# Router logits of a hybrid block: token activations as the stationary operand, 36 router columns moving

## The chip, the core and the metric

The kernel runs on one core of one Trainium2 chip. The metric is the device time of one execution in microseconds (us), as the median of several runs. The profile is one execution, recorded by the hardware profiler.

## What is computed

One decoder block on 256 tokens of width 1024, in float32. A gated short convolution and an attention run on the same input, are merged and projected (`mix`); then a layer norm, a hierarchical mixture of experts and a second layer norm follow. Cut to what matters here:

```python
x = layer_norm(alpha * x + mix, ln1_g, ln1_b)
g_prob = softmax(xt @ w_router_group)                 # (256, 4)
g_top_p, g_top = top_k(g_prob, 1)
e_logits = (xt @ w_router_expert).reshape(-1, 4, 8)   # (256, 32)
e_top_logit, e_top = top_k(e_logits[g_top], 2)        # two experts inside the group
...
h = silu(xt @ w_gate[e]) * (xt @ w_up[e]) * combine   # 32 experts, width 256
ffn = h @ w_down[e]
x = layer_norm(alpha * x + ffn, ln2_g, ln2_b)
```

The router is a product of the (256, 1024) activations with 4 + 32 = 36 columns.

## The kernel before

The 256 tokens are two tiles (`TT = 2`) of 128, and the width 1024 is eight chunks (`KC = 8`) of 128. Everything is written out by hand for each engine, and the engines meet at semaphores; an engine takes its instructions in the order of the program.

**Up to the router.** TensorE (PE) computes the projections; the mix is added up in banks 0 to 3 of PSUM (`merge`, L1366), and ScalarE (ACT) copies it out as `zx` (L760), tokens on partitions. VectorE (DVE) takes mean and variance, GpSimd (POOL) the reciprocal root `rstd`. The first layer norm is not applied before the router: its gain and bias are folded into the router's weights `wr` (36 columns with the gain, then 36 with the bias), and the mean is brought in by `offs`, so that a logit is `rstd * (zx @ wr) + offs`.

**The router.** `transpose_tile` (L1398) turns `zx` into chunks with channels on partitions, in banks 4 and 5 for tile 0 and 6 and 7 for tile 1; four copies on ACT (L765) make `x1T` of them and count `bank_free[4]` to `bank_free[7]`. `logit_parts(t)` (L1409) then loads 36 columns of `wr` for each chunk as the stationary operand and moves 128 tokens of `x1T` past them. Even chunks are summed in partitions 0 to 35 of bank `4 + t`, odd ones in partitions 64 to 99 (`APART_AT`), so the result lies with logits on partitions and in two parts. `take_parts` (L1003, DVE) copies it to `lT`, and `logits` (L1416, PE) multiplies `lT` as the stationary operand by `both`, two shifted pieces of the identity added together, which turns the result back to tokens on partitions and adds the two parts. L1037 (DVE) reads that and adds `offs`.

**Behind the router.** DVE finds the best group and two experts in a chain of short instructions (L1021 to L1052), PE counts ranks (L1435), DVE makes one-hot selections `pick` (L1070), and PE starts the experts: gather with `pick` (L1450), gate and up products (L1501), down product (L1537), scatter (L1549), in quads of four experts, eight quads. Between L1416 and L1435 PE also zeroes the four sums (`zero_sums`, L1242) and runs nine products for warmth (L1303).

**Loads.** All large loads go through one queue in SyncE's (SP) order. At the router this is, from the code:

```python
sp.wait_ge(acc_done, 2 * TT)
load_gu(1, 1, [3], parts=[1])
sp.wait_ge(parts_ps, TT)
load_gu(1, 1, [2], parts=[1])
sp.wait_ge(offs_read, TT)
load_dn_early(3, slice(0, 1))
sp.wait_ge(x1p_done, TT)
load_gu(1, 1, [0], parts=[0])
```

The tile `gu` for the next quad and `dn_r` overlay tiles that the router still uses (`x1T`, `wr`, `offs`), which is why these loads wait. `x1p` (L771, ACT) is the normalized activation, for the gather. After that SP waits for `rounds_done` and for `gate_ps`, counted by the first gate products, to refill the buffer of quad 0 with quad 2's weights in three pieces (L533), then for `gu_ps` and `y_ps` of each quad.

Of the kernel before, what the change touches and what calls it, by code (L numbers as in the profile page):

```python
# [27 lines left out]
ALU = mybir.AluOpType  # L28
# [3 lines left out]
P = 128  # L32
SEQ, DM = 256, 1024
TT = SEQ // P
# [41 lines left out]
def hybrid_block(nc, x, w_in, conv_w, w_out_conv, w_out_attn, w_o, ln1_g, ln1_b,  # L76
# [18 lines left out]
    with ctx:  # L95
        def sb(name, shape, dt=F32, where=ctx):
            return where.enter_context(nc.sbuf_tensor(name, shape, dt))

        def sem(name):
            return ctx.enter_context(nc.semaphore(name))  # L100
# [92 lines left out]
        y_scope.close()  # L193
        lT_scope = ExitStack()
        lT = sb("lT", [P, TT, P], where=lT_scope)
        lT_scope.close()
        xg_scope = ExitStack()
# [55 lines left out]
        rounds_f = sb("rounds_f", [P, 4, 16], where=route_scope)  # L253
        both = sb("both", [P, NL], where=route_scope)
        route_scope.close()
# [81 lines left out]
        x1T_ps = sem("x1T_ps")  # L337
        parts_ps = sem("parts_ps")
        lT_done = sem("lT_done")
        logit_ps = sem("logit_ps")  # L340
# [50 lines left out]
        UPJ = 8  # L391
        APART_AT = P // 2
        AHEAD = NSPL - 2
# [18 lines left out]
        def _(sp):  # L412
# [103 lines left out]
            load_gu(1, 1, [3], parts=[1])  # L516
            sp.wait_ge(parts_ps, TT)
            load_gu(1, 1, [2], parts=[1])
# [305 lines left out]
        def _(dve):  # L824
# [70 lines left out]
            def scale_router():  # L895

                dve.wait_ge(consts, N_CONSTS)
                dve.wait_ge(small_in, N_SMALL)
                dve.tensor_tensor(both[:, :], ident[:, 0:NL], ident[:, APART_AT:APART_AT + NL], ALU.add)
                for v, cols in ((wrg, slice(0, NG)), (wre, slice(NG, NL))):  # L900
# [98 lines left out]

            def take_parts(t):  # L1000

                dve.wait_ge(parts_ps, t + 1)
                dve.tensor_copy(lT[:, t, :], bank[4 + t][:, 0:P]).then_inc(lT_done, 1)  # L1003

            take_parts(0)
            dve.wait_ge(neg_mean_done, 1)
            dve.wait_ge(bias_read, 1)
            for t in range(TT):
                ins = dve.scalar_tensor_tensor(offs[:, t, :], rsum_b[:, 0:NL], neg_mean[:, t:t + 1],
                                               rsum_b[:, NL:2 * NL], ALU.mult, ALU.add)  # L1010
            take_parts(1)
            link(ins)
# [21 lines left out]
            gtop, tmp, gsum, w1, w2 = (rs[:, i, :] for i in range(5))  # L1034
            dve.wait_ge(logit_ps, 1)
            for t in range(TT):
                ins = dve.scalar_tensor_tensor(logit[:, t, :], bank[4][:, t * NL:(t + 1) * NL],  # L1037
                                               rstd[:, t:t + 1], offs[:, t, :], ALU.mult, ALU.add
                                               ).then_inc(offs_read, 1)
# [153 lines left out]
        def _(pe):  # L1193
# [208 lines left out]

            def logit_parts(t):

                for k in range(KC):
                    if t and k % KHALF == 0:
                        pe.wait_ge(bank_free[6 + k // KHALF], 1)
                    at = APART_AT * (k % 2)
                    mm = pe.matmul(bank[4 + t][at:at + NL, 0:P], wr[:, k, 0:NL], x1T[:, k, t * P:(t + 1) * P],  # L1409
                                   start=(k < 2), stop=(k >= KC - 2), skip_group_check=True)  # L1410
                mm.then_inc(parts_ps, 1)

            def logits(t):

                pe.wait_ge(lT_done, t + 1)
                return pe.matmul(bank[4][:, t * NL:(t + 1) * NL], lT[:, t, :], both[:, :],  # L1416
                                 start=True, stop=True, skip_group_check=True)

# [3 lines left out]
            for b in (4, 5):  # L1422
                pe.wait_ge(bank_free[b], 1)
            logit_parts(0)
            logit_parts(1)
            logits(0)
            logits(1).then_inc(logit_ps, 1)
            pe.wait_ge(moment_done, TT)
# [186 lines left out]
```

## Time and profile before

| | |
|---|---|
| median of 3 runs | 391.53 us (391.07 to 392.49) |
| profiled execution | 391.15 us |
| its span, first to last instruction | 388.7 us |
| outside the span | 2.45 us |
| PE busy | 359.8 us (93%) |
| DVE busy | 161.4 us (42%) |
| ACT busy | 138.6 us (36%) |
| HBM read | 131.25 MB, 340 GB/s over the span |

The busy share of PE is an average over stages with different limits, and it includes products that only keep the engine warm. An engine name "PEld" is the load of the stationary operand, which the profile lists apart from the product. One float32 product is two records on PE and two on PEld where it is a true product, so `x32` at L1409 is 16 products; a transpose is one record.

### The profile page before, as it was taken

How to read it: one execution, taken by the hardware profiler on the slowest of the kernel's cores; microseconds unless marked ns; L12 is line 12 of the kernel's file. 1: busy time of each engine (PE TensorE's matmuls, PEld its weight loads, DVE VectorE, ACT ScalarE, POOL GpSimd, SP SyncE). 2: the span in 40 equal slices, each digit the busy share in tenths (PEclk: the TensorE clock that was granted, in tenths of full speed). 3: DMA queues.
4: the chain of work that ended last, by engine and by line, in shares of the span. 5: the costliest groups of instructions: out<-in, count | busy, mean ns of one | idle time of the engine just before them, and what ended most of it. 6: DMA issues, size and time to landing. Idle time of an engine off the chain costs nothing.

```text
span 388.7 us, 8033 instructions
## 1 busy us (share of the span) xinstructions
PE 359.8 (93%) x3336; PEld 285.8 (74%) x3336; DVE 161.4 (42%) x336; ACT 138.6 (36%) x240; POOL 35.2 (9%) x42
## 2 busy tenths in 40 slices
PE   7999999999999999999999999999599598299995
PEld 6999988999999999998657575656256356157642
DVE  3546579787365666464731202030510112011135
ACT  4643565655535453435723131322111213012012
POOL 3310000000000000001000005208720000000001
PEclk9999999999999999999999999999799899599999
DMA  8699884966859879799899999999999999999962
GB/s 284 211 329 375 292 303 156 337 221 218 275 177 316 274 265 376 239 389 368 311 385 429 424 427 425 417 420 427 427 420 414 427 426 426 427 424 429 411 256 110
DMA packets 52053, 132.79 MB, mean 342 GB/s; under 512 B 2818, under 2 KB 36626, under 8 KB 41012
## 3 DMA queue, kind: packets, MB, share of 16 engines
q1 hardware_dynamic: 51572, 131.88, 87.9%
q8 instruction: 26, 0.43, 0.4%
q0 software_dynamic: 304, 0.17, 0.4%
q10 hardware_dynamic: 144, 0.26, 0.2%
q14 instruction: 7, 0.06, 0.0%
HBM read 131.25 MB, written 1.05 MB: 340 GB/s over the span
## 4 chain that ended last, share of the span: by engine, by line
PE 70%; DMA 13%; DVE 6%; SPq 4%; issue 3%; ACT 3%; DVEq 0%
PE bank L1204 15%; PE bank L1501 13%; PE bank L1233 7%; DMA gu<-in_w_up 7%; PE bank L1537 7%; PE bank L1366 6%; PE bank L1450 6%; PE bank L1549 6%; DMA raw<-in_w_in 5%; SPq L470 4%; PE bank L1236 3%; DVE wl L837 3%; PE bank L1303 2%; ACT wh L655 1%; PE bank L1520 1%
## 5 line engine op out<-in xcount | busy, mean ns | idle before, releaser
L837 DVE TENSOR_TENSOR wl<-raw,wh 128x1024 fp32r<-128x1024 f32 x54 | 65.8, 1223 | 54.6 <-ACT wh L655 54.5
L1501 PE MATMUL bank<-gu,xg 128*32 128x256 f32 x1024 | 63.4, 407 | 17.8 <-issue 17.7
L655 ACT ACTIVATE wh<-raw 128x1024 fp32r<-128x1024 f32 x54 | 56.5, 1056 | 61.2 <-DMA raw<-in_w_in 23.4
L1501 PEld LDWEIGHTS bank<-gu,xg 128*32 128x32 f32 x1024 | 35.0, 117 | 42.5 <-issue 23.8
L1233 PE MATMUL bank<-xh,wh 128*128 128x256 f32 x176 | 44.1, 288 | 0.1
L1233 PE MATMUL bank<-xl,wh 128*128 128x256 f32 x176 | 43.1, 283 | 0.0
L1233 PEld LDWEIGHTS bank<-xh,wh 128*128 128x128 f32 x176 | 33.6, 191 | 2.3 <-issue 2.0
L1101 DVE TENSOR_SCALAR xg<-bank,gcol,bcol 128x128 f32<-128x128 f32 x32 | 11.7, 406 | 53.6 <-PE bank L1450 53.6
L1233 PEld LDWEIGHTS bank<-xl,wh 128*128 128x128 f32 x176 | 33.7, 191 | 0.0
L1450 PEld LDWEIGHTS bank<-pick,x1p 128*128 128x128 f32 x256 | 29.9, 192 | 2.4 <-issue 1.3
L1450 PE MATMUL bank<-pick,x1p 128*128 128x128 f32 x256 | 30.5, 276 | 0.7 <-DVE pick L1070 0.7
L1549 PE MATMUL bank<-ys,put 128*128 128x256 f32 (+1 forms) x96 | 30.0, 461 | 0.7 <-ACT ys L796 0.7
L1549 PEld LDWEIGHTS bank<-ys,put 128*128 128x128 f32 x96 | 17.4, 189 | 13.6 <-issue 10.1
L1204 PE MATMUL bank<-xh,wl 128*128 128x256 f32 x96 | 27.2, 283 | 0.0
L1204 PE MATMUL bank<-xl,wh 128*128 128x256 f32 x96 | 27.2, 283 | 0.0
L1204 PE MATMUL bank<-xh,wh 128*128 128x256 f32 x96 | 27.2, 283 | 0.0
L780 ACT ACTIVATE xg<-bank,bcol,gcol 128x128 f32<-128x128 f32 x32 | 13.7, 456 | 34.5 <-PE bank L1450 34.5
L1537 PE MATMUL bank<-dn,hT 128*32 128x256 f32 (+1 forms) x324 | 25.9, 453 | 0.0
L1236 PE MATMUL bank<-xh,wl 128*128 128x256 f32 x176 | 24.7, 283 | 0.0
L1236 PEld LDWEIGHTS bank<-xh,wl 128*128 128x128 f32 x176 | 22.7, 192 | 0.0
L1127 DVE TENSOR_TENSOR sg<-sg,bank 128x256 f32<-128x256 f32 x8 | 3.4, 421 | 41.7 <-ACT sg L786 41.7
L786 ACT ACTIVATE sg<-bank 128x256 f32<-128x256 f32 x8 | 3.1, 384 | 48.1 <-PE bank L1501 48.1
(228 smaller groups left out, 586.6 us busy)
## 6 DMA issues: line engine op xcount, KB each, us to landing
gu<-in_w_up SPq DMA_DIRECT2D x31, 1024.0 KB, 19.0
gu<-in_w_gate SPq DMA_DIRECT2D x30, 1024.0 KB, 14.5
dn<-in_w_down SPq DMA_DIRECT2D x26, 1024.0 KB, 17.7
raw<-in_w_in SPq DMA_DIRECT2D x40, 512.0 KB, 5.2
raw<-in_w_o SPq DMA_DIRECT2D x8, 512.0 KB, 4.4
raw<-in_w_out_conv SPq DMA_DIRECT2D x4, 512.0 KB, 4.2
raw<-in_w_out_attn SPq DMA_DIRECT2D x4, 512.0 KB, 5.5
gu<-in_w_gate SPq DMA_DIRECT2D x1, 2048.0 KB, 9.9
```

The costliest lines, as they stand in the source:

```text
L470: sp.dma_start(gu[(NQ - 1) % 2][:, e, c, ks, :], (wg_v, wu_v)[c][:, (NQ - 1) * QE + e, ks, :]).then_inc(last_up_end if i else last_gu_in[c ...
L655: act.activation(wh[:, s, :].rearrange("p (k c) -> p k c", k=KC), raw[pair % NRAW][:, :].rearrange("p (k c) -> p k c", k=KC) [:, :, n % 2 ...
L780: act.activation(xg[:, k, :], bank[XG_BANK[i]][:, (k - lo) * P:(k - lo + 1) * P], ACT.Identity, scale=gcol[:, k:k + 1], bias=bcol[:, k:k + ...
L837: dve.tensor_tensor(wl[:, s, :].rearrange("p (k c) -> p k c", k=KC), raw[pair % NRAW][:, :].rearrange("p (k c) -> p k c", k=KC) [:, :, n % ...
L1204: mm = pe.matmul(dst, w[:, k, :], v[:, i, :], start=(i == 0 and w is h and v is high_in), stop=(i == len(ks) - 1 and w is l))
L1233: pe.matmul(dst, h[:, k, :], v[:, k, :], start=(k == 0 and v is xh), stop=False)
L1236: mm = pe.matmul(dst, l[:, k, :], xh[:, k, :], start=False, stop=(k == KC - 1))
L1366: mm = pe.matmul(bank[2 * t + h][:, :], v[:, m, t * P:(t + 1) * P], w[:, s, h * HALF:(h + 1) * HALF], start=(j == 0 and m == 0 and i == 0) ...
L1450: mm = pe.matmul(bank[XG_BANK[i]][:, (k - lo) * P:(k - lo + 1) * P], x1p[:, t, k, :], pick[:, t, :, :].rearrange("p e s -> p (e s)"), star ...
L1501: mm = pe.matmul(bank[6 - part][g, 0:DE], xg[:, k, g], w[:, e, part, k, :], start=(k == 0), stop=(k == KC - 1), skip_group_check=True)
L1537: mm = pe.matmul(bank[b][g, 0:hi - lo], hT[:, j, g], dn_of(q, e)[:, j, lo:hi], start=(j == 0), stop=(j == FC - 1), skip_group_check=True)
L1549: pe.matmul(bank[2 * t + lo // HALF][:, lo % HALF:lo % HALF + hi - lo], put[:, t * P:(t + 1) * P], ys[:, lo:hi], start=False, stop=True, s ...
```

## The change

`logit_parts`, `take_parts`, `lT` and `both` are gone. `logits(t)` now takes a chunk of `x1T` (128 channels, 128 tokens) as the stationary operand and moves the 36 columns of `wr` past it. The eight products of a tile add up in one place, the first 36 columns of bank `4 + t`, with tokens on partitions already. `logit_ps` is counted once per tile, and both SP's load and DVE wait for both tiles.

```diff
-        lT_scope = ExitStack()
-        lT = sb("lT", [P, TT, P], where=lT_scope)
-        lT_scope.close()
...
-        both = sb("both", [P, NL], where=route_scope)
...
-        APART_AT = P // 2
...
-            sp.wait_ge(parts_ps, TT)
+            sp.wait_ge(logit_ps, TT)
             load_gu(1, 1, [2], parts=[1])
...
-                dve.tensor_tensor(both[:, :], ident[:, 0:NL], ident[:, APART_AT:APART_AT + NL], ALU.add)
...
-            def take_parts(t):
-
-                dve.wait_ge(parts_ps, t + 1)
-                dve.tensor_copy(lT[:, t, :], bank[4 + t][:, 0:P]).then_inc(lT_done, 1)
-
-            take_parts(0)
             dve.wait_ge(neg_mean_done, 1)
             dve.wait_ge(bias_read, 1)
             for t in range(TT):
                 ins = dve.scalar_tensor_tensor(offs[:, t, :], rsum_b[:, 0:NL], neg_mean[:, t:t + 1],
                                                rsum_b[:, NL:2 * NL], ALU.mult, ALU.add)
-            take_parts(1)
             link(ins)
...
-            dve.wait_ge(logit_ps, 1)
+            dve.wait_ge(logit_ps, TT)
             for t in range(TT):
-                ins = dve.scalar_tensor_tensor(logit[:, t, :], bank[4][:, t * NL:(t + 1) * NL],
+                dve.scalar_tensor_tensor(logit[:, t, :], bank[4 + t][:, 0:NL],
                                                rstd[:, t:t + 1], offs[:, t, :], ALU.mult, ALU.add
                                                ).then_inc(offs_read, 1)
...
-            def logit_parts(t):
+            def logits(t):
 
                 for k in range(KC):
                     if t and k % KHALF == 0:
                         pe.wait_ge(bank_free[6 + k // KHALF], 1)
-                    at = APART_AT * (k % 2)
-                    mm = pe.matmul(bank[4 + t][at:at + NL, 0:P], wr[:, k, 0:NL], x1T[:, k, t * P:(t + 1) * P],
-                                   start=(k < 2), stop=(k >= KC - 2), skip_group_check=True)
-                mm.then_inc(parts_ps, 1)
-
-            def logits(t):
-
-                pe.wait_ge(lT_done, t + 1)
-                return pe.matmul(bank[4][:, t * NL:(t + 1) * NL], lT[:, t, :], both[:, :],
-                                 start=True, stop=True, skip_group_check=True)
+                    mm = pe.matmul(bank[4 + t][:, 0:NL], x1T[:, k, t * P:(t + 1) * P], wr[:, k, 0:NL],
+                                   start=(k == 0), stop=(k == KC - 1))
+                mm.then_inc(logit_ps, 1)
...
-            logit_parts(0)
-            logit_parts(1)
             logits(0)
-            logits(1).then_inc(logit_ps, 1)
+            logits(1)
```

On PE, between the transposes and the warm products, the order before is this. The shape at the end of a row is stationary columns by moving columns.

```order
L1398 MATMUL bank<-ident,zx 128x128 x7
L1409 MATMUL bank<-x1T,wr 36x128 [waits bank_free5,bank_free4]
L1409 MATMUL bank<-x1T,wr 36x128 x7
L1409 MATMUL bank<-x1T,wr 36x128 [waits bank_free6]
L1409 MATMUL bank<-x1T,wr 36x128 x3
L1409 MATMUL bank<-x1T,wr 36x128 [waits bank_free7]
L1409 MATMUL bank<-x1T,wr 36x128 x3
L1416 MATMUL bank<-both,lT 128x36 [waits lT_done] x2
L1242 MATMUL bank<-zeros_b 128x512 [waits moment_done]
```

The same place on PE in the changed kernel:

```order
L1383 MATMUL bank<-ident,zx 128x128 x7
L1393 MATMUL bank<-wr,x1T 128x36 [waits bank_free5,bank_free4]
L1393 MATMUL bank<-wr,x1T 128x36 x7
L1393 MATMUL bank<-wr,x1T 128x36 [waits bank_free6]
L1393 MATMUL bank<-wr,x1T 128x36 x3
L1393 MATMUL bank<-wr,x1T 128x36 [waits bank_free7]
L1393 MATMUL bank<-wr,x1T 128x36 x3
L1227 MATMUL bank<-zeros_b 128x512 [waits moment_done]
```

The count of 16 products and their waits stay; the shape turns round, and the two products that waited for `lT_done` are gone. On DVE, from the mean to the first step behind the logits, before:

```order
L996 SCALAR_TENSOR_TENSOR neg_mean<-moments,rstd 128x2 [waits rstd_done]
L1003 COPY lT<-bank 128x128 [waits parts_ps]
L1009 SCALAR_TENSOR_TENSOR offs<-rsum_b,neg_mean 128x36 [waits bias_read,neg_mean_done]
L1009 SCALAR_TENSOR_TENSOR offs<-rsum_b,neg_mean 128x36
L1003 COPY lT<-bank 128x128 [waits parts_ps]
L1037 SCALAR_TENSOR_TENSOR rt<-bank,rstd,offs 128x36 [waits logit_ps,dve_link]
```

And in the changed kernel:

```order
L988 SCALAR_TENSOR_TENSOR neg_mean<-moments,rstd 128x2 [waits rstd_done]
L995 SCALAR_TENSOR_TENSOR offs<-rsum_b,neg_mean 128x36 [waits bias_read,neg_mean_done]
L995 SCALAR_TENSOR_TENSOR offs<-rsum_b,neg_mean 128x36
L1022 SCALAR_TENSOR_TENSOR rt<-bank,rstd,offs 128x36 [waits logit_ps,dve_link]
L1022 SCALAR_TENSOR_TENSOR rt<-bank,rstd,offs 128x36
```

Both copies are gone and nothing takes their place. On SP's queue, the loads around the router in the changed kernel:

```order
L428 DMA gu<-in_w_up 128x2048 [waits acc_done]
L428 DMA gu<-in_w_up 128x2048 [waits logit_ps]
L433 DMA dn_r<-in_w_down 128x1024 [waits offs_read]
L428 DMA gu<-in_w_gate 128x2048 [waits x1p_done]
L519 TENSOR_LOAD bounds [waits rounds_done]
```

Before, the second of these rows read `[waits parts_ps]`; the others and their order are the same.

## Rows read from the trace of the kernel before

**Rows 1.** The page's first line.
```profile
span 388.7 us, 8033 instructions
```

**Rows 2.** Chain that ended last, router stage: start us, us, what.
```profile
182.98 1.90 PE bank L1409 x32
...
184.90 0.30 DVE lT L1003
...
185.25 0.43 PE bank L1416 x2
...
185.77 0.43 DVE rt L1037 x2
...
188.59 0.43 PE bank L1435 x10
...
189.73 0.73 PE bank L1450 x4
```

**Rows 3.** The same chain, later.
```profile
272.92 4.73 issue
...
338.15 26.18 DMA gu<-in_w_up
```

**Rows 4.** Timeline, router stage: start us, us, engine line operation.
```profile
182.14 1.58 ACT L765 ACTIVATE x1T<-bank 128x512 f32<-128x512 f32 x3
...
182.91 1.68 PEld L1409 LDWEIGHTS bank<-x1T,wr 128*36 128x36 f32 x32
...
184.05 4.38 ACT L771 ACTIVATE x1p<-zx,neg_mean,rstd 128x1024 f32<-128x1024 f32 x2 [0.32 <-DVE neg_mean L996]
184.24 0.41 DVE L1009 SCALAR_TENSOR_TENSOR offs<-rsum_b,neg_mean 128x36 f32<-128x36 f32 x2
184.78 0.30 PEld L1416 LDWEIGHTS bank<-both,lT 128*128 128x128 f32 x2 [0.20 <-issue]
...
184.90 0.33 SPq L435 DMA_DIRECT2D gu<-in_w_up  x1
...
186.36 2.17 PE L1303 MATMUL bank<-ident 128*128 128x128 f32 x18
```

**Rows 5.** Single lines: ns min/median/max, first and last start.
```profile
L1416 PEld LDWEIGHTS bank<-both,lT x4: 186/188/189, 184.8 to 185.4; 128*128 128x128 f32 x4
...
L1303 PE MATMUL bank<-ident x106: 273/275/582, 1.8 to 371.1; 128*128 128x128 f32 x106
...
L1435 PE MATMUL bank<-hot,ones_b x6: 176/176/177, 188.7 to 188.8; 128*128 128x32 bf16 x6
```

**Rows 6.** SP's queue in order of time.
```profile
181.17 4.06 SPq L435 DMA_DIRECT2D gu<-in_w_up  x2
186.22 0.33 SPq L440 DMA_DIRECT2D dn_r<-in_w_down  x1
188.46 0.33 SPq L435 DMA_DIRECT2D gu<-in_w_gate  x1
192.20 0.39 SPq L533 DMA_DIRECT2D gu<-in_w_gate  x1
```

**Rows 7.** Stretches: busy us, PEclk, DMA share, GB/s.
```profile
186.50:187.00 0.50, 0.50 (x7) 0.50 (x6) 0.44 (x3) 0.50 (x1) 0.00 (x0) 1.00 0.68 213
...
189.00:192.00 3.00, 2.18 (x25) 1.28 (x24) 2.56 (x14) 1.85 (x4) 0.00 (x0) 1.00 0.83 264
...
200.00:270.00 70.00, 69.03 (x796) 44.37 (x789) 12.28 (x40) 16.86 (x35) 13.81 (x5) 1.00 1.01 423
270.00:374.00 104.00, 84.33 (x904) 53.79 (x902) 18.14 (x48) 18.24 (x38) 11.40 (x7) 0.90 1.01 422
374.00:389.00 15.00, 10.37 (x54) 4.61 (x54) 7.96 (x15) 2.78 (x6) 1.15 (x2) 1.00 0.30 113
```

**Rows 8.** DVE's timeline, early in the kernel.
```profile
35.81 0.19 DVE L899 TENSOR_TENSOR both<-ident 128x36 f32<-128x36 f32 x1
...
40.04 2.45 DVE L837 TENSOR_TENSOR wl<-raw,wh 128x1024 fp32r<-128x1024 f32 x2 [1.88 <-ACT wh L655]
```

More of the change, by code:

```diff
@@ L337, in hybrid_block @@
         x1T_ps = sem("x1T_ps")
-        parts_ps = sem("parts_ps")
-        lT_done = sem("lT_done")
         logit_ps = sem("logit_ps")
```

## The prediction

> **What bounds the kernel now.** The page first: one span of 388.7 us [rows 1], which the profiled execution's 391.15 us exceeds by 2.45 us for what lies outside the first and the last instruction. Then I read the kernel in stretches [rows 7]. The reader is to see three regimes. From 200 to 374 us the DMA engines are at a share of 1.01 and move 422 to 423 GB/s without a break. From 374 us on the share is 0.30, and TensorE, VectorE and the output share the tail. Before 200 us there are holes, one of them at the router: 213 GB/s at 186.5 us, and 264 GB/s on average from 189 to 192 us. The chain of work that ended last confirms the middle regime: TensorE stands still 4.73 us at 272.9 us, and the chain runs through a transfer of `in_w_up` for 26.18 us at 338 us [rows 3]. So behind 200 us the end is set by bytes, and a delay of TensorE at the router counts in so far as it pushes the stream of loads back. All loads behind the router are released by something in it, so the chain there has to be read next [rows 2], and then SP's queue [rows 6].
>
> In that chain, 16 products (L1409) end at 184.88 us, the second copy of `lT` starts at 184.90, the two records of the second L1416 start at 185.25, and VectorE reads the logits at 185.77 us (L1037). From there to the first gather at 189.73 us nothing but short steps of VectorE and PE follow each other.
>
> **What goes.** The first load of L1409 starts at 182.91 us [rows 4], the logits are read at 185.77 us [rows 2]: 2.86 us for the router's products, copy and turning back. All of it is replaced. Behind the last product of L1409 the chain loses 185.77 - 184.88 = 0.89 us: the copy, the product that turns back, and their handovers.
>
> **What comes.** 16 products in the same place, 32 records as before, but each loads 128 columns of `x1T` and moves 36, where before it loaded 36 and moved 128, in two halves of the array side by side. How long a record of the new shape takes is the one term that decides. The trace has this shape once: L1416, 128 by 36 in float32. Its two loads together cover 0.30 us [rows 4] and one takes 0.188 us [rows 5], so the second starts 0.11 us behind the first. Loads of 128 columns followed by 128 moving columns (L1303) come out alike: 18 records in 2.17 us, less 0.275 us for the last, over 17 is 0.111 us [rows 4, 5]. That the spacing is the same with 36 moving columns as with 128 says that the load sets it. L1409 itself took (1.68 - 0.11) / 31 = 0.05 us a record [rows 4], since its two halves ran together and its loads were short.
>
> I take 0.11 us. From the first load to the last are 31 steps, 3.41 us. From the last load's start to VectorE's read is what L1416 shows: 185.77 - 185.25 = 0.52 us for two records, less one step, 0.41 us [rows 2]. Together 3.82 us against 2.86 us: **the logits come 0.96 us later**, at 186.73 us. The start stays at 182.91 us: the transposes and the two first copies of `x1T`, which it waits for, are untouched. The last copy of `x1T` ends at 182.14 + 1.58 = 183.72 us [rows 4], when the new stream is still in tile 0 (which takes 16 x 0.11 = 1.76 us), so no product waits for it.
>
> The bounds of that step: below, the bf16 products L1435, whose 10 records of 128 by 32 take 0.43 us [rows 2], less 0.176 us [rows 5], over 9, 0.028 us each. Above, load and product one after the other: 0.11 us plus the time of 36 moving columns, at most 0.11 x 36/128 = 0.03 us, 0.14 us. The row nearest in shape and type is L1416, so the value stays at 0.11 us. The clock was granted in full (1.00) here [rows 7], and PE has no pause in the new form, so I set nothing for it.
>
> A rule of the Trainium skill stands beside this. TensorE: Matmul & The Clock Gate, under Back-to-back issue gap, gives about 81 ns for a pair of load and product at 128 moving columns in a sustained stream. The float32 rows above at 0.11 us do not show that; by the rule 31 x 0.081 + 0.41 = 2.92 us, the logits would come 0.06 us later, and the change would cost nothing.
>
> **The edits that I set at nothing.** `both` is made at 35.81 us in 0.1 us of VectorE's time (0.19 us with its overlap); VectorE's next large step at 40.04 us had waited 1.88 us for ScalarE [rows 8], which hides it; without that cover it would be 0.1 us. The first copy of `lT` stood ahead of `offs` on VectorE; `offs` may now start some 0.2 us earlier than 184.24 us [rows 4] and is ready long before 186.73 us. ScalarE's `x1p` runs from 184.05 to 188.43 us [rows 4] and hangs on the mean, not on the logits; the gather waited until 189.73 us for `pick`, so 1.3 us of slack there grows. `zero_sums` and the warm products sit behind the logits on PE and move with them by the same 0.96 us, so they end as far ahead of the ranks (L1435) as before.
>
> **From the router to the end.** Everything behind the logits on PE, the first gate products included, comes 0.96 us later. What is the stream's own delay? Queued on SP behind the changed wait are three loads and the refills. The load that waited for L1409 was issued at 184.90 us [rows 4]; it now waits for the last product, 182.91 + 3.41 + 0.32 (0.41 less the 0.09 us from the product's end at 185.68 to VectorE's read) + 0.02 = 186.66 us, 1.76 us later. Before, the stream was back at about 186.7 us [rows 7], 1.8 us behind the issue; now 188.5 us. The three loads are 128 x 2048, 128 x 1024 and 128 x 2048 floats, 2.62 MB, 6.2 us at 423 GB/s: done at 194.7 us. The next load is the first refill, issued at 192.20 us [rows 6] and now at 193.16 us, flowing 1.8 us later, at 195.0 us. So the three loads close up (the trace wastes (1 - 264/423) x 3 = 1.1 us between 189 and 192 us, which they use), and the refill sets the stream's delay: 0.96 us, as on PE. Behind it every load is released by a product that is 0.96 us later, or waits behind bytes that are.
>
> **The sum:** + 3.41 + 0.41 - 2.86 = +0.96 us, on the profiled execution 391.15 + 0.96 = 392.1 us. That execution lies 0.38 us under the median of 391.53 us; against the median the change gives **392.5 us**. What a measurement of this kernel tells from no change is about 0.5%, 1.96 us, so I forecast no change that can be told.
>
> **The rivals.**
>
> *The products take turns with their loads (slower).* If a load of 128 columns cannot run beside the product ahead of it, a step is 0.14 us: 31 x 0.14 + 0.41 = 4.75 us, the logits 1.89 us later. The first held-back load would flow at 189.4 us and the three be done at 195.6 us, the refill at 192.20 + 1.89 + 1.8 = 195.9 us, so the stream too is 1.9 us late: 393.4 us. From (2.86 + 1.96 - 0.41) / 31 = 0.142 us a step it is slower by over 0.5%. For it: L1303 cannot tell it for a short moving side. Against it: the spacing in L1416.
>
> *The loads are quick (faster).* With steps of 0.028 us the second half of tile 1 waits for the copy at 183.72 us, then 8 x 0.028 + 0.41: 184.35 us; `offs` is then last, at about 184.45 us, and the logits come 1.3 us earlier. `x1p` at 188.43 us just lets the gather start that much earlier. The refill is issued at 190.9 us and flows at 192.7 us, when the load released by `x1p` (issued 188.46 us, flowing at 190.3 us, 2.5 us long) is through: 390.2 us. The step from which the change gains is (2.86 - 0.41) / 31 = 0.079 us. For it: L1435 is 128 columns wide as well. Against it: that is bf16, and both float32 rows say 0.11 us. The Trainium skill has a rule for the difference: TensorE: Matmul & The Clock Gate, under Fast Weight Load, says that the quick load is on for 128 weights only where the type is not FP32. The two kinds of rows agree with it, and it speaks against this rival.
>
> *The stream hides it.* If the refill's lateness is covered by bytes still in flight, the delay is that of the first load less the 1.1 us won back, 1.76 - 1.1 = 0.6 us, or less: 391.5 to 392.1 us. For it: the hole at 189 to 192 us. Against it: the refill's own issue is 0.96 us later, and the three loads would be done before it flows.
>
> **How the numbers follow.** Load-bound steps and the whole delay 0.73, the stream hides most 0.10, quick loads 0.09, taking turns 0.08. The likeliest gives 392.5 us. Two in ten left out at the ends: the low end cuts off most of the quick loads and keeps the hidden case, less a few tenths for the spread of runs (391.07 to 392.49 us around the median), 391.2 us; the high end takes in taking turns with 0.3 us for the same spread, 393.7 us. Faster by over 0.5% (under 389.6 us) needs quick loads and luck, 0.03; slower by over 0.5% (over 393.5 us) is half of taking turns and a little from the spread, 0.06; within it 0.91.
>
> **What would show it.** In the changed kernel's profile: 32 loads of the new line with about 3.6 us from the first's start to the last's end (1.68 us before); VectorE's read of the logits at 186.7 us; the held-back load of `in_w_up` issued at 186.7 us, and the first refill at 193.2 us; DMA at 1.01 from 200 to 375 us as before. A wrong step length shows in the first of these, a hidden delay in a refill at 193.2 us with the idle time at 272.9 us shortened and the end unmoved. The prediction is wrong if the spacing of the loads is not that of L1416, or if the loads that open the long stream do not follow PE.

## Result, and the profile after

| | before | changed |
|---|---|---|
| median | 391.76 us (20 runs, 390.25 to 392.62) | 393.36 us (20 runs, 391.19 to 396.79) |
| ratio to before | | 1.0050, 95% interval 1.0035 to 1.0064 |
| profiled execution, span | 391.15, 388.7 us | 394.32, 391.4 us |

The change costs time: 1.4 to 2.5 us by the interval, 1.60 us by the medians, where the sum had 0.96 us. The direction, and the 0.96 us at the router, are as worked out ahead. The median is 0.9 us above the forecast 392.5 us; 0.23 us of that lies in the kernel before, which was at 391.53 us in the forecast and is at 391.76 us here. The interval leaves out "no change", which was forecast. The two profiled executions differ by 2.7 us in span, more than the medians do: the executions counted here lie up to 2.4 us apart before and 5.6 us after, so a span from one trace is weak evidence. What can be compared is a distance between two events inside the same stage.

The page of the changed kernel, its first line and the busy times:

```profile
span 391.4 us, 8022 instructions
...
PE 363.1 (93%) x3332; PEld 288.3 (74%) x3332; DVE 160.3 (41%) x333; ACT 138.7 (35%) x240; POOL 35.1 (9%) x42
```

The chain that ended last, at the router (start us, us, what); it answers to [rows 2].

```profile
181.67 1.85 PE bank L1383 x16
183.51 3.66 PE bank L1393 x32
...
187.26 0.43 DVE rt L1022 x2
...
190.09 0.43 PE bank L1411 x10
...
191.22 0.73 PE bank L1426 x4
```

From the products' start on the chain to the reading of the logits it is 187.26 - 183.51 = 3.75 us; before it was 185.77 - 182.98 = 2.79 us [rows 2]. That is 0.96 us more. Behind the logits nothing changed: to the gather it is 191.22 - 187.26 = 3.96 us, and 189.73 - 185.77 = 3.96 us before.

The timeline of the changed kernel there, which answers to [rows 4] (start us, us, engine, line, operation):

```profile
182.20 2.06 ACT L758 ACTIVATE x1T<-bank 128x512 f32<-128x512 f32 x4
...
183.39 3.65 PEld L1393 LDWEIGHTS bank<-wr,x1T 128*128 128x128 f32 x32
183.43 3.73 PE L1393 MATMUL bank<-wr,x1T 128*128 128x36 f32 x32
...
187.26 0.42 DVE L1022 SCALAR_TENSOR_TENSOR rt<-bank,rstd,offs 128x36 f32<-128x36 f32 x2 [2.26 <-PE bank L1393]
```

And one line of it by itself (ns min/median/max):

```profile
L1393 PEld LDWEIGHTS bank<-wr,x1T x32: 186/192/192, 183.4 to 186.8; 128*128 128x128 f32 x32
```

The 32 loads take 3.65 us, less 0.19 us for the last, over 31: 0.112 us a step. VectorE waits 2.26 us for them, and ScalarE's copies end at 184.26 us, long before the last chunk is needed.

SP's queue, which answers to [rows 6]:

```profile
181.70 5.82 SPq L428 DMA_DIRECT2D gu<-in_w_up  x2
187.71 0.33 SPq L433 DMA_DIRECT2D dn_r<-in_w_down  x1
188.97 0.33 SPq L428 DMA_DIRECT2D gu<-in_w_gate  x1
193.71 0.39 SPq L526 DMA_DIRECT2D gu<-in_w_gate  x1
```

From the logits to the first refill: 193.71 - 187.26 = 6.45 us; 192.20 - 185.77 = 6.43 us before [rows 2, 6]. The refill is late by what the logits are late.

Stretches, with the columns: us, busy of PE, PEld, DVE, ACT and POOL (x instructions), granted clock, DMA share, GB/s. They answer to [rows 7].

```profile
187.00:189.00 2.00, 2.00 (x17) 1.62 (x17) 1.53 (x9) 1.98 (x2) 0.00 (x0) 1.00 0.38 74
189.00:192.00 3.00, 2.22 (x27) 1.93 (x26) 2.54 (x17) 1.49 (x3) 0.00 (x0) 1.00 0.94 375
200.00:270.00 70.00, 69.02 (x813) 43.86 (x806) 12.70 (x41) 17.32 (x36) 13.15 (x5) 1.00 1.01 422
270.00:374.00 104.00, 85.86 (x905) 55.38 (x903) 17.52 (x48) 17.80 (x37) 11.97 (x7) 0.90 1.01 422
374.00:392.00 18.00, 11.94 (x69) 4.86 (x62) 8.01 (x15) 3.38 (x7) 1.15 (x2) 0.96 0.35 130
```

The hole has moved to 187 to 189 us (74 GB/s), and the three held-back loads close up (375 GB/s from 189 to 192 us, 264 before). From 200 to 374 us the stream runs at the same 422 GB/s.

One thing was not in the forecast. VectorE in the tail of the changed kernel, between two steps that wait for no other engine:

```profile
382.23 0.15 DVE L974 TENSOR_SCALAR moments<-moments 128x1 f32<-128x1 f32 x1
382.71 0.70 DVE L1153 BATCH_NORM_STATS2 stats<-bank 128x6 f32<-128x512 f32 x1 [0.33 <-issue]
```

The same two steps in the kernel before:

```profile
380.13 0.15 DVE L982 TENSOR_SCALAR moments<-moments 128x1 f32<-128x1 f32 x1
380.23 0.70 DVE L1168 BATCH_NORM_STATS2 stats<-bank 128x6 f32<-128x512 f32 x1
```

In the changed kernel the engine is idle 0.33 us for "issue", in which it waits for nothing that the profile shows. The two starts lie 0.48 us apart, where they lay 0.10 us apart: the tail is 0.38 us longer, and this piece is on the chain that ended last.

The start of the last quad's gate and up products splits the rest of the execution. On the chain of the kernel before and of the changed kernel it is:

```profile
365.99 3.63 PE bank L1501 x64
```

```profile
368.07 3.63 PE bank L1477 x64
```

With it the 2.7 us between the two spans come apart. The router's first load is 0.48 us later (182.91 and 183.39 us), before anything that the change touches; among the kernels with the old products this start lies anywhere from 182.85 to 184.15 us. From there to the first refill it is 1.03 us more (9.29 and 10.32 us), which is the router's part. From the refill to the last quad it is 0.57 us more (173.79 and 174.36 us), and from there to the end of the span 0.6 us more (22.7 and 23.3 us), which holds the pause.

### The profile page after: what moved, and what is told of

It is laid out like the page before. It is cut to its first block, busy times and chain, and to the rows that moved or that the text cites. A ratio compares the mean times of both kernels' runs of the same rounds, so it can differ in the third digit from the quotient of the medians.

```text
span 391.4 us, 8022 instructions
## 1 busy us (share of the span) xinstructions
PE 363.1 (93%) x3332; PEld 288.3 (74%) x3332; DVE 160.3 (41%) x333; ACT 138.7 (35%) x240; POOL 35.1 (9%) x42
## 3 DMA queue, kind: packets, MB, share of 16 engines
HBM read 131.25 MB, written 1.05 MB: 338 GB/s over the span
## 4 chain that ended last, share of the span: by engine, by line
PE 76%; DMA 9%; DVE 5%; SPq 4%; issue 3%; ACT 2%; DVEq 0%; ACTq 0%
PE bank L1189 15%; PE bank L1477 13%; PE bank L1218 8%; DMA gu<-in_w_up 7%; PE bank L1513 7%; PE bank L1351 6%; PE bank L1426 6%; PE bank L1525 5%; PE bank L1221 4%; SPq L463 3%; PE bank L1333 3%; PE bank L1288 2%; DMA raw<-in_w_in 2%; DVE wl L830 2%; ACT wh L648 1%
## 5 line engine op out<-in xcount | busy, mean ns | idle before, releaser
L1477 PE MATMUL bank<-gu,xg 128*32 128x256 f32 x1024 | 64.8, 414 | 16.8 <-issue 16.7
L1477 PEld LDWEIGHTS bank<-gu,xg 128*32 128x32 f32 x1024 | 35.8, 119 | 42.1 <-issue 23.9
L1221 PEld LDWEIGHTS bank<-xh,wl 128*128 128x128 f32 x176 | 22.7, 192 | 0.0
```

What stands on the lines that cost most here:

```text
L1221: mm = pe.matmul(dst, l[:, k, :], xh[:, k, :], start=False, stop=(k == KC - 1))
L1477: mm = pe.matmul(bank[6 - part][g, 0:DE], xg[:, k, g], w[:, e, part, k, :], start=(k == 0), stop=(k == KC - 1), skip_group_check=True)
```

## The experiments

All ratios are to the kernel before, timed beside it on the same chip, with a 95% interval. 1.0025 is 0.96 us. A ratio is not the quotient of the two medians; where the two tell different sizes, the text gives both.

### How large is the remainder?

The changed kernel was timed twice more, unchanged.

> The changed kernel once more, unaltered. Theory A (a fixed delay at the router, carried to the end by the stream of loads): 1.0 to 1.6 us over the kernel before, with the same spread as that one. Theory B (the router's delay of about 1 us plus, in some executions, a lower granted clock in the last stretch): the median 1.3 to 2 us over, single executions 3 us and more over, and those with a mean granted clock of 0.969 or less instead of about 0.973.

Measured: 393.66 us, 1.0038 (1.0018 to 1.0059). What the expectation says of the mean granted clock falls: an execution at 0.966 took 392.73 us and one at 0.973 took 394.78 us.

> The changed kernel a third time, beside its padded form. Program-length theory: 1.5 to 1.9 us over the kernel before, with the idle time of 0.33 us ahead of L1153 in the profile. Theory that the products have a price of their own: the same total.

Measured: 393.69 us, 1.0039 (1.0020 to 1.0057). The pause of 0.33 us ahead of the last statistics is in both traces. The mean over the three timings is 1.0042, +1.7 us. So 0.96 us of the router is more than half, and 0.7 us are left. Each interval reaches 0.6 to 0.8 us to either side, so the 0.7 us are themselves known only roughly.

### Do the loads set the step?

```diff
-                    mm = pe.matmul(bank[4 + t][:, 0:NL], x1T[:, k, t * P:(t + 1) * P], wr[:, k, 0:NL],
+                    mm = pe.matmul(bank[4 + t][:, 0:2 * NL], x1T[:, k, t * P:(t + 1) * P], wr[:, k, :],
```

Twice the columns are moved, and the upper 36 results are read by nobody.

> The changed kernel with all 72 columns of wr moving instead of 36; the upper 36 results are not read. Load-bound theory: the 32 records start 0.11 us apart as with 36 columns, the stage takes the same 3.65 us of loads. Taking turns (load, then product): 0.03 us more a record, 1.0 us more in all.

> The changed kernel with 72 columns moved instead of 36 (the upper 36 results are not read), now timed. In the trace of the changed kernel with two memsets moved to GpSimd, TensorE's granted clock fell to half at about 186.9 us, right behind the router's products, and the warm products took 3.43 instead of 2.17 us; no other trace shows it. Theory that such a fall comes in part of the executions of the changed kernel, because its router products keep the array less busy, and makes up what 0.96 us do not explain: with twice the columns the fall is rarer, the ratio to the kernel before drops to about 1.0025 (+0.96 us). Rival, that the fall is chance and the remainder has another source (the tail's pause of 0.33 us, and scatter): 1.0035 to 1.0045, as for the changed kernel, and the step between loads 0.11 us as in the first look.

This kernel ran once by itself (393.24 us) and was then timed: 393.23 us, 1.0037 (1.0018 to 1.0055). Its chain and its loads in the timed run:

```profile
183.94 3.69 PE bank L1393 x32
...
187.72 0.43 DVE rt L1022 x2
```

```profile
183.82 3.65 PEld L1393 LDWEIGHTS bank<-wr,x1T 128*128 128x128 f32 x32
```

The loads take 3.65 us with 72 columns as with 36, and the stage 187.72 - 183.94 = 3.78 instead of 3.75 us. Up to 72 columns the moved side costs nothing that shows: the float32 load of 128 columns sets the step. The rival in which products and loads take turns is out; with it 36 more columns would have cost 31 x 0.03 = 0.9 us.

### What carries the delay: PE, or the held-back load?

First the load alone. In the kernel before, it now waits until VectorE has read `offs` and the logits of both tiles (`offs_read`), instead of for `parts_ps`:

```diff
-            sp.wait_ge(parts_ps, TT)
-            load_gu(1, 1, [2], parts=[1])
             sp.wait_ge(offs_read, TT)
+            load_gu(1, 1, [2], parts=[1])
             load_dn_early(3, slice(0, 1))
```

> The kernel before with only the held load moved: it waits for the logits to be read instead of for the products of L1409, so it is issued about 1.3 us later and PE is left alone. Refill theory (as predicted: the three loads close up and the first refill, released by the gate products, sets the stream's delay): 0 to 0.3 us. Held-load theory (the hole that opens at the held load is not won back): 1.0 to 1.4 us.

Measured: 391.90 us, 0.9997 (0.9980 to 1.0013). The load's lateness costs nothing.

Then PE alone: warm products between the parts and the turning back.

```diff
             logit_parts(1)
+            stay_warm(6)
             logits(0)
```

> The kernel before with six warm products (12 records, 1.3 us of PE) between the products of L1409 and those of L1416: the logits come about 1.0 us later, the held load is issued as before at 184.9 us. Refill theory: 1.0 us. Held-load theory: 0 to 0.4 us, since the first of the three loads is in time and the others fill the hole less late.

Measured: 392.57 us, 1.0024 (1.0008 to 1.0040). The logits are 1.09 us later in its trace, the refill follows them at 6.43 us, and the time rises by 0.9 us.

Then both:

```diff
-            sp.wait_ge(parts_ps, TT)
+            sp.wait_ge(logit_ps, 1)
             load_gu(1, 1, [2], parts=[1])
...
             logit_parts(1)
+            stay_warm(6)
             logits(0)
```

> The kernel before, with the six warm products between the products of L1409 and those of L1416 (logits about 1.0 us later) and the held load waiting for the last product of L1416 (about 2.7 us later). It has the changed kernel's timing on both engines without its shape of products. Together theory (the late load and late PE add up, because the three loads are then not through when the refill comes): 1.6 to 2.0 us, as the changed kernel. Refill theory (only PE's lateness counts): 0.9 to 1.1 us, and then the changed kernel's remainder of some 0.7 us belongs to its products.

Measured: 392.50 us, 1.0006 (0.9989 to 1.0024), +0.25 us with up to 0.94 us inside the interval. By the medians it is 0.76 us above the kernel before. The interval overlaps that of PE alone, and the two runs don't say that the load adds to PE's delay. By this ratio alone the 1.1 us could also have arrived in part; the traces below decide that better.

Last, the load freed in both kernels: `x1T` in two halves and `offs` lie where no load lands, and SP issues the load right behind the one ahead of it.

```diff
+        xa_scope = ExitStack()
+        x1Ta = sb("x1Ta", [P, KHALF, SEQ], where=xa_scope)
+        xa_scope.close()
...
+        xb_scope = ExitStack()
+        x1Tb = sb("x1Tb", [P, KHALF, SEQ], where=xb_scope)
...
             load_gu(1, 1, [3], parts=[1])
-            sp.wait_ge(logit_ps, TT)
             load_gu(1, 1, [2], parts=[1])
```

> The changed kernel with x1T in two other places (the halves that yh, yl and sig leave free), so that the held load needs no logits and is issued right behind the one before it; PE is as in the changed kernel, logits 1.0 us late. Together theory: 0.9 to 1.1 us over the kernel before. Refill theory with a price of the products themselves: still 1.6 to 1.9 us.

> The kernel before with the same relocation: the held load is issued some 3.5 us earlier, PE unchanged. Refill theory: 0 us (-0.2 to 0.2), since the three loads were through before the refill came. Held-load theory: 0.5 to 1.2 us faster, the hole from 185.4 to 186.7 us being filled.

Measured: the changed kernel 393.77 us, 1.0044 (1.0024 to 1.0064); the kernel before with the same edit 392.54 us, 1.0001 (0.9982 to 1.0021). Its median is 0.80 us above that of the kernel before (391.74 us), which the ratio does not show. By either measure freeing the load wins nothing back in either kernel, so the remainder does not come from it.

A larger dose of the delay on PE, `stay_warm(15)` in the same place:

> The kernel before with fifteen warm products (30 records, 3.3 us of PE) where pe_late had six: the logits come about 3.1 us later than before. Proportional theory (the stream of loads passes on PE's lateness at the router one for one): 2.8 to 3.3 us. Theory that the stream passes on only a part (as pe_late and both_late could be read, 0.2 to 0.9 us for 1.1): 1.2 to 2.4 us.

Measured: 394.44 us (6 runs), 1.0076 (1.0047 to 1.0104), +3.0 us. From its chain:

```profile
183.02 1.87 PE bank L1409 x32
184.89 3.54 PE bank L1303 x30
188.44 0.38 PE bank L1416 x4
...
188.91 0.43 DVE rt L1037 x2
```

The stage is 188.91 - 183.02 = 5.89 us, 3.10 us more than before, and 3.0 us arrive at the end. The interval of this time is wide (1.8 to 4.1 us) and would by itself allow that only six tenths arrive. The trace says more. Its first refill and its last quad:

```profile
195.35 0.39 SPq L533 DMA_DIRECT2D gu<-in_w_gate  x1
```

```profile
369.32 3.63 PE bank L1502 x64
```

From the refill to the last quad it is 369.32 - 195.35 = 173.97 us, with the refill 3.15 us later, against 365.99 - 192.20 = 173.79 us in the kernel before; the other two delayed forms have 173.54 (PE alone) and 173.79 us (both). So the stretch behind the refill does not shrink when the refill is late. A delay of the logits is carried to the end one to one, within what is measured.

### The pause in the tail

The changed kernel has fewer instructions on VectorE, 333 busy ones (the page above). Three instructions that do nothing were put back:

```diff
                 dve.wait_ge(small_in, N_SMALL)
+                dve.engine_nop()
...
+            dve.engine_nop()
+            dve.engine_nop()
             link(ins)
```

> The changed kernel with three instructions that do nothing on VectorE, one where both was made and two behind offs, so that VectorE's program is as long as before (242 rows instead of 239). PE's products and SP's waits are the changed kernel's. Program-length theory: VectorE's idle time of 0.33 us, put down to issue, ahead of L1153 in the last stretch is gone, the stretch from the last bn_stats of bank 1 to the end is 0.4 us shorter, and the kernel costs 1.0 to 1.3 us over the kernel before instead of 1.5 to 1.9. Theory that the products have a price of their own: the idle time may go or stay, the total stays at 1.7 us.

> The padded form of the changed kernel a second time (three do-nothing instructions on VectorE). Program-length theory: 0.4 us less than the changed kernel beside it, 1.1 to 1.5 us over the kernel before, and no idle time ahead of the last bn_stats. Theory of a price of the products: no less than the changed kernel beside it.

> The changed kernel with three do-nothing instructions on VectorE, a third time, beside the other two. If 0.96 us at the router is all, 1.0025; if something of 0.3 to 0.4 us is left that is no pause in the tail, 1.0033 to 1.0038 as twice before. No pause ahead of the last statistics in its trace.

The pause is gone in all three traces. From the first of them:

```profile
381.43 0.15 DVE L975 TENSOR_SCALAR moments<-moments 128x1 f32<-128x1 f32 x1
381.53 0.70 DVE L1156 BATCH_NORM_STATS2 stats<-bank 128x6 f32<-128x512 f32 x1
```

The time: 1.0038 (1.0021 to 1.0055), 1.0033 (1.0011 to 1.0056), 1.0046 (1.0027 to 1.0065), mean 1.0039, against 1.0042 unpadded. The traces say that 0.38 us of the tail is the pause's; the times do not tell the two forms apart, and 0.38 us is 0.1%, less than any of these intervals. So the pause is shown in the traces, and its share of the remainder is not shown by the time. What the traces add: from the last quad's products to the end of the span it is 23.0 to 23.3 us in all six traces with the pause, and 22.6 to 22.8 us in all nine of the old products and in four of the five changed ones without it. The fifth, the second padded one, has 24.2 us, with the extra time behind VectorE's last step.

Can the kernel before be made to pause? Two trims:

```diff
-                    act.wait_ge(z_done, c + 1)
+                    if c == 0:
+                        act.wait_ge(z_done, 1)
+                    else:
+                        act.wait_ge(evac_v, evacuated(n)[1])
```

> The kernel before with three of VectorE's four do-nothing instructions behind the convolution's product taken out (ScalarE waits for that product's own count instead), so VectorE's program is as short as the changed kernel's (239 rows), and the router is untouched. Program-length theory: the idle time of 0.33 us ahead of the last bn_stats appears here too, and the kernel is 0.3 to 0.5 us slower than before. Other theory: no idle time there, 0 us.

Measured: 392.04 us, 1.0006 (0.9988 to 1.0024), no pause. Its trace still has 8033 instructions, so it did not test what it was made for.

```diff
-            dve.memset(rounds_f[:, :, :], 0.0)
-            link(dve.memset(u_t[:, :, 0:2], 0.0))
...
-                dve.tensor_tensor(both[:, :], ident[:, 0:NL], ident[:, APART_AT:APART_AT + NL], ALU.add)
...
+            const(pool.memset(rounds_f[:, :, :], 0.0))
+            const(pool.memset(u_t[:, :, 0:2], 0.0))
+            pool.wait_ge(ident_done, 1)
+            const(pool.tensor_tensor(both[:, :], ident[:, 0:NL], ident[:, APART_AT:APART_AT + NL], ALU.add))
```

> The kernel before with three real instructions taken off VectorE's program near its start (two memsets and the making of both, now on GpSimd), the router untouched. In the first attempt at this the do-nothing instructions had been replaced by others that wait, so the program had not become shorter (8033 instructions recorded, as before). Program-length theory: the idle time of 0.33 us ahead of the last bn_stats appears, and the kernel is 0.3 to 0.5 us slower. Otherwise: no idle time, 0 us.

> The kernel before with two memsets and the making of both moved from VectorE to GpSimd, a second time: it came out 1.0 us faster. If the move has a real effect: again 0.6 to 1.6 us faster. If builds of the same router scatter by some tenths of a per cent without a cause in it: 0, or a sign that changes.

Measured: 390.90 us, 0.9974 (0.9959 to 0.9990), and 391.22 us, 0.9986 (0.9965 to 1.0007). No pause, so the theory that fewer instructions on VectorE bring it by themselves is not borne out. But here is the fastest version of the study: three small steps moved from VectorE to GpSimd take 0.5 to 1.0 us off the kernel before, clearly in one timing and not clearly in the other.

The same move in the changed kernel (it has no `both`):

> The changed kernel with the same two memsets moved to GpSimd. If the move has a real effect: 1 us less than the changed kernel, 0.5 to 1.0 us over the kernel before. If not: 1.5 to 1.9 us over the kernel before.

> The changed kernel with two memsets moved to GpSimd, again. If the fall of TensorE's clock to half at 186.9 us belongs to this recorded program, it is in this trace too, and the first refill is issued 7.8 us behind the reading of the logits; if it comes by chance from execution to execution, the trace most likely has 6.44 us like the others. The time: 1.0025 to 1.0035.

Measured: 392.27 us, 1.0031 (1.0009 to 1.0053), and 392.24 us, 1.0012 (0.9994 to 1.0030), no pause in either. That is faster than the changed kernel by about as much as the move gave before, and no version of the changed kernel beats the kernel before. These forms are also a second pair without a pause on either side. The first of them was timed beside the second timing of the moved form of the kernel before: 392.27 and 391.22 us, 1.05 us apart by the medians and about 1.8 us (1.0031 and 0.9986) by the ratios. So with the pause absent on both sides the change still costs something between the router's 0.96 us and the whole 1.7 us, and these timings can't say which.

### A half clock behind the router

The first of these two traces held something new. Behind the router the first refill is issued 7.84 us behind the logits, where nine of the eleven traces of changed forms show 6.43 to 6.45 us. Its stretches there (columns as above) and its PE:

```profile
183.00:186.00 3.00, 3.00 (x29) 3.00 (x29) 0.72 (x4) 2.68 (x3) 0.56 (x1) 1.00 0.74 306
186.00:187.00 1.00, 1.00 (x9) 0.73 (x9) 0.31 (x2) 1.00 (x2) 0.00 (x0) 0.94 0.00 0
187.00:190.00 3.00, 3.00 (x14) 2.67 (x12) 2.52 (x17) 2.79 (x3) 0.00 (x0) 0.50 0.74 262
190.00:191.00 1.00, 1.00 (x12) 0.99 (x11) 0.00 (x0) 0.08 (x1) 0.00 (x0) 0.86 0.85 352
```

```profile
187.66 3.43 PE L1288 MATMUL bank<-ident 128*128 128x128 f32 x18
```

The granted clock falls from 1.00 to 0.50, from the 2.4 to the 1.2 GHz level, for some 3.4 us. PE had not paused ahead of it: it was busy 3.00 of 3.00 us with the router's products. The 18 warm products, which take 2.17 us at full clock [rows 4], take 3.43 us, the ranks wait for them, and the refill is 1.4 us late. The third padded trace shows the same, as the clock column of its stretches says:

```profile
183.00:186.00 3.00, 3.00 (x29) 3.00 (x29) 0.58 (x3) 2.68 (x4) 0.56 (x1) 1.00 0.72 306
...
187.00:190.00 3.00, 3.00 (x14) 2.77 (x13) 2.39 (x16) 2.72 (x3) 0.00 (x0) 0.50 0.79 276
```

It is not bound to a recorded program: the same kernels run again, or recorded before, have 1.00 there. It is in 2 of 11 traces of the changed forms and in none of 9 of the forms with the old products, which is not enough to say that the new products bring it. If they do, 2/11 x 1.4 to 1.5 us would add 0.3 us on average. The timed run with 72 columns was to tell: by the theory on record the falls would have become rarer and the ratio 1.0025. It gave 1.0037, but the interval holds both. Whether the fall belongs to the change stays open.

### Why single executions scatter

In some traces the chain behind 330 us does not run through the last transfer of `in_w_up`, but through PE. From the chain of the first repetition of the changed kernel:

```profile
330.50 7.83 issue
338.33 9.78 PE bank L1477 x128
...
367.11 3.63 PE bank L1477 x64
```

128 records in 9.78 us, where the last quad takes 3.63 us for 64, 7.26 us for as many. PE had stood still for 7.83 us, for which the profile names no releaser (a load is likely, since the DMA engines are busy throughout), and came back at a granted clock of 0.50 from 338 to 341 us. The kernel before has the same pause and the same 0.50 there, and takes 8.94 us for its 128 records. The same chain is in traces of both kernels (the kernel before with its load freed, and the one with `stay_warm(6)`, show it too). How little slack PE has at the last load shows its timeline in the kernel before:

```profile
364.38 1.60 PE L1303 MATMUL bank<-ident 128*128 128x128 f32 x12 [0.26 <-DMA gu<-in_w_up]
```

It waits only 0.26 us there, so full clock that returns a microsecond sooner or later there can move the end by fractions of a microsecond. That is argued from the slack and not tested. The chain is in three of nine traces of the old products and in three of eleven of the new, so it looks like scatter of both kernels and no part of the difference.

## Why the prediction was right in its main term and wrong in its verdict

**What failed.** Two steps. The first is the limit that turned the sum into a verdict: "What a measurement of this kernel tells from no change is about 0.5%, 1.96 us". With 20 runs on each side the interval came out from 1.4 to 2.5 us, 0.3% wide, and a loss of 0.96 us lies outside an interval of that width around zero too. So "no change that can be told" did not even follow from its own sum. The second is the sum: behind the router it had nothing but the 0.96 us, and the three timings give 1.7 us on average. Of the 0.7 us left out, the traces show 0.38 us in VectorE's tail; the cause of the rest stays open.

**What comes: right.** "I take 0.11 us": 0.112 us measured. "3.82 us" from the first load to the logits: 187.26 - 183.39 = 3.87 us. "The logits come 0.96 us later": 3.87 - 2.86 = 1.01 us from the first load, as the forecast counted, and 0.96 us on the chain. The rivals of the step fall: taking turns (0.14 us a step) by the run with 72 columns, quick loads (0.028 us) by the 3.65 us of the loads. The Trainium skill (TensorE: Matmul & The Clock Gate, under Back-to-back issue gap) gives about 81 ns for a pair of load and product at 128 moving columns; the float32 rows of this case, 0.111 us with 128 moving columns and 0.112 us with 36, don't agree with it.

**From the router to the end: right, and tested.** The stream's delay is the refill's. The refill comes 6.45 us behind the logits (6.43 before), the three held-back loads closed up, the held-back load alone, later or earlier, changes nothing that is told (0.9997, 1.0001), 3.10 us of delay gave 3.0 us, and the stretch behind the refill was as long with it as without. "The stream hides it" falls with that.

**The edits that I set at nothing: here the sum falls short.** The sum was 0.96 us, and three timings of the changed kernel give 1.7 us on average. One mechanism of the 0.7 us is seen: the pause of 0.33 us ahead of the last statistics. It is in all six traces in which VectorE's program is that of the changed kernel (three of it as it is, one with its load freed, two with 72 columns), and in none of nine of the forms before. The step asked only what cover each removed instruction had in its own place. It did not ask what else shifts with the program. It is a place where the trace shows time lost, but padding it away did not move the time measurably (1.0039 against 1.0042), so most of the 0.7 us need not be the pause's.

**"PE has no pause in the new form, so I set nothing for it": not safe.** In 2 of 11 traces the clock fell to half right behind the new products without any pause, at a price of 1.4 us. Whether that is more frequent than before could not be settled.

**The chances.** 0.91 stood on "no change that can be told", and it fell with the limit of 0.5%. The stated 391.2 to 393.7 us holds the 393.36 us, but not for its reasons alone: its high end had been set to take in the products that take turns, which the runs rule out.

**Open.** Of 0.7 us above the router's 0.96, 0.38 us are accounted for by the pause in the traces alone, 0.3 us could be the half clock, and neither was isolated by time. Why the pause comes is open too. The cause of the gain from moving three steps to GpSimd wasn't looked for further.

## What to carry to other kernels

When one side of a float32 product is short, look at what the other side's load costs: the swap to a 128-column stationary side made each record 0.112 instead of 0.05 us, and 32 of these cost more than the copy and turning back (0.89 us) that they saved. Where loads are released by a chain and the stream behind is saturated, as here from 200 to 374 us, a delay of that chain reached the end one to one, and one of a load that merely waits in between did not. Work out from earlier runs how narrow the interval will be before calling a cost too small to be seen. Differences of 0.3 us need more than one build of each kernel: put a do-nothing instruction in as a control, and look in the tail for idle time put down to "issue".

## What the runs showed of the hardware

- VectorE can stand 0.33 us between two steps in order without any semaphore. A block of 8 KB of the queue of kind "instruction" moves nearby, and its place goes with the program: 1.2 to 1.6 us ahead of the start of the last statistics in the padded forms and in seven of the nine forms with the old products, 0.6 to 1.0 us behind it in the six traces with the pause, and 1.0 to 1.2 us behind it in the four with steps moved to GpSimd, which have no pause. In the traces with the pause it thus moves when the pause is over (at 383.4 us in the changed kernel, whose last statistics start at 382.71 us), so VectorE can't simply have waited for this block. What the pause is was not found, and leaving out instructions alone did not bring it.
- The granted clock can fall to half although PE is busy without a gap (3.00 of 3.00 us ahead of it), here for 3.4 us behind 16 products with a short moving side, in 2 of 11 traces.
- The length of a float32 step with 128 loaded columns is the same with 36, 72 and 128 moving columns: 0.11 us (L1393, the run with 72 columns, and L1303).
